# Values as the stationary operand, and inverse sums through diagonal matrices, in one attention of a two-block kernel

## The reference, cut to what matters

```python
def dense_attn(q, k, v):
    Bq, Lq, Hq, dh = q.shape
    Hk = k.shape[2]
    qg = q.reshape(Bq, Lq, Hk, Hq // Hk, dh)
    s = jnp.einsum('bqkgd,bskd->bkgqs', qg, k).astype(jnp.float32) * (dh ** -0.5)
    p = jax.nn.softmax(s, axis=-1).astype(v.dtype)
    o = jnp.einsum('bkgqs,bskd->bqkgd', p, v)
    return o.reshape(Bq, Lq, Hq * dh)
...
    y_b = blocked_attn(q, jnp.concatenate([ck, k], axis=1), jnp.concatenate([cv, v], axis=1))
    y_a = conformer_conv(a_val, a_gate, conv_w, conv_b, ln_g, ln_b)
    y = jnp.concatenate([y_a, y_b], axis=-1) * jax.nn.silu(z)
    x = x + gate * (y @ w_out)
```

## Time and profile before

| what | value |
|---|---|
| median of 3 runs | 1135.54 us (1134.69 to 1135.82) |
| profiled execution, its time | 1135.69 us |
| its span | 1133.9 us |
| TensorE busy | 1097.7 us, 97% |
| VectorE busy | 750.8 us, 66% |
| ScalarE busy | 550.6 us, 49% |
| GpSimd busy | 44.5 us, 4% |
| granted TensorE clock, mean | 0.995 |

### The profile page before, as it was taken

One profiled execution on the slowest core, in us unless ns is written; L12 is line 12 of the kernel. 1 busy time (PEld: TensorE's weight loads), 2 busy tenths in 40 slices (PEclk: granted clock), 3 DMA queues, 4 the chain that ended last, 5 costly groups with the idle time before them and its releaser, 6 DMA issues. The chain is left out here.

```text
span 1133.9 us, 17977 instructions
## 1 busy us (share of the span) xinstructions
PE 1097.7 (97%) x7052; PEld 948.2 (84%) x7052; DVE 750.8 (66%) x1456; ACT 550.6 (49%) x986; POOL 44.5 (4%) x55
## 2 busy tenths in 40 slices
PE   8999999999999999999999999999999999999996
PEld 6877879899887877889999988898876887989865
DVE  4765756655555566776888888789777653834475
ACT  5543845444444543855444444435457623623273
POOL 1000001000000000000000000100300000000000
PEclk9999999999999999999999999999999999999999
DMA  9668055555554568045556546343335037864000
GB/s 340 236 207 307 2 154 181 177 194 187 186 180 160 186 193 321 2 149 188 167 192 206 188 161 200 102 149 112 110 140 187 2 112 261 196 171 138 30 18 39
DMA packets 52536, 182.30 MB, mean 161 GB/s; under 512 B 18661, under 2 KB 31333, under 8 KB 32869
## 3 DMA queue, kind: packets, MB, share of 16 engines
q1 hardware_dynamic: 52452, 181.16, 48.5%
HBM read 178.26 MB, written 2.89 MB: 160 GB/s over the span
## 5 line engine op out<-in xcount | busy, mean ns | idle before, releaser
L224 DVE TENSOR_TENSOR w_lo<-ring,w_hi 128x1024 fp32r<-128x1024 f32 x260 | 317.1, 1224 | 214.1 <-ACT w_hi L218 211.5
L218 ACT CAST w_hi<-ring 128x1024 fp32r<-128x1024 f32 x260 | 271.5, 1052 | 323.1 <-PE banks L280 319.1
L280 PE MATMUL banks<-shared_hi,w_hi 128*128 128x256 f32 (+1 forms) x448 | 134.0, 299 | 0.0
L280 PE MATMUL banks<-shared_lo,w_hi 128*128 128x256 f32 (+1 forms) x448 | 133.7, 298 | 0.0
L280 PE MATMUL banks<-shared_hi,w_lo 128*128 128x256 f32 (+1 forms) x448 | 133.6, 298 | 0.0
L280 PE MATMUL banks<-w_hi,u_hi 128*128 128x512 f32 x256 | 100.6, 393 | 0.0
L280 PE MATMUL banks<-w_lo,u_hi 128*128 128x512 f32 x256 | 100.4, 392 | 0.0
L280 PE MATMUL banks<-w_hi,u_lo 128*128 128x512 f32 x256 | 100.3, 392 | 0.0
L280 PEld LDWEIGHTS banks<-shared_hi,w_lo 128*128 128x128 f32 x448 | 85.7, 191 | 2.6
L280 PEld LDWEIGHTS banks<-shared_hi,w_hi 128*128 128x128 f32 x448 | 85.7, 191 | 2.5
L280 PEld LDWEIGHTS banks<-shared_lo,w_hi 128*128 128x128 f32 x448 | 85.7, 191 | 2.4
(11 more groups left out here) (401 smaller groups left out, 2257.0 us busy)
## 6 DMA issues: line engine op xcount, KB each, us to landing
ring<-in_w_up SPq DMA_DIRECT2D x32, 1024.0 KB, 5.1
ring<-in_w_down SPq DMA_DIRECT2D x32, 1024.0 KB, 5.1
ring<-in_w_in SPq DMA_DIRECT2D x24, 1024.0 KB, 6.4
ring<-in_ab_ada SPq DMA_DIRECT2D x12, 1024.0 KB, 5.2
ring<-in_cd_ada SPq DMA_DIRECT2D x12, 1024.0 KB, 5.1
ring<-in_cd_in SPq DMA_DIRECT2D x12, 1024.0 KB, 8.9
ring<-in_w_out SPq DMA_DIRECT2D x8, 1024.0 KB, 6.9
ring<-in_ab_in SPq DMA_DIRECT2D x16, 512.0 KB, 4.8
```

What stands on the lines that cost most here:

```text
L218: nc.scalar.copy(w_hi[:, n % PARTS, :], part_source(key, q)).then_inc(hi_ready, 1)
L224: nc.vector.tensor_tensor(w_lo[:, n % PARTS, :], part_source(key, q), w_hi[:, n % PARTS, :].bitcast(F32), ALU.subtract).then_inc(part_read ...
L280: mm = nc.tensor.matmul(dst, a, b, start=first_one and i == 0, stop=last_one and i == 2, skip_group_check=shares_bank)
```

## The change

A new function, `attend_by_feature`, takes the place of `attend` in this one stage. What it does otherwise:

- The units are put in another order: two halves of 12, and in each the four heads of one group of tokens follow each other.
- Turning a piece is now a product: the probabilities' piece is stationary, and a 128x128 diagonal matrix with the inverse row sums moves. So the turned probabilities come out scaled. GpSimd makes the diagonal: the identity times the inverse sums, broadcast along the row; three such matrices are held, each with room for two row groups.
- The values are stationary (64 columns), and the turned, scaled probabilities move. Units i and i + 2, two heads with the same values, write to the lower and the upper 64 partitions of one bank. The result stands with features on the partitions, so nothing is left to transpose.
- TURN is 3 and VALUES 8; 4 probabilities and 6 turned ones are held; ten products of `keep_busy` stand behind the first four scores.
- VectorE no longer scales products. After the first half it gates banks 6 and 7 (features 0 and 2); the second half's are gated in `out_project`.
- "ab_out" now stands in `next_key`: its first two parts of weights are split at the end of the attention. `out_project` has no transposes, its two gates read banks 6 and 7, and casts and subtractions follow.

```diff
-        next_key = {"ab_out": "cd_in", "cd_in": "cd_out", ("ffn", DEPTH - 1): "ab_in"}
+        next_key = {"attended": "ab_out", "ab_out": "cd_in", "cd_in": "cd_out", ("ffn", DEPTH - 1): "ab_in"}
...
-                    if attended is not None:
-                        for g in range(4):
-                            for t in range(4):
-                                mm = nc.tensor.transpose(banks[:, 4 + g, t * P:(t + 1) * P],
-                                                         mixed[:, t, BANK + g * P:BANK + (g + 1) * P], ident[:])
-                            mm.then_inc(turned_here, 1)
-                    else:
+                    if attended is None:
...
-                        act.wait_ge(gate_done, g + 1)
+                        if g % 2 == 1:
+                            act.wait_ge(gate_done, g // 2 + 1)
...
-                        dve.wait_ge(turned_here, g + 1)
-                        nc.vector.scalar_tensor_tensor(out=gated_y[g], in0=banks[:, 4 + g, :], scalar=0.5, in1=silu_z[g],
+                        nc.vector.scalar_tensor_tensor(out=gated_y[g], in0=banks[:, 6 + g // 2, :], scalar=0.5, in1=silu_z[g],
...
+        def attend_by_feature(units, probs, probsT, diagonals, finals, gate_chunk, aside, aside_scalar, next_key):
...
+            SCALE, TURN, VALUES = 2, 3, 8
...
+                    def turn(i):
+                        pe.wait_ge(probs_ready, i + 1)
+                        pe.wait_ge(diagonal_ready, i + 1)
+                        if i >= 2:
+                            pe.wait_ge(turned_copied, i - 1)
+                        for r, (_, _, c0, n, _, _) in enumerate(units[i]["rows"]):
+                            for c in range(c0, c0 + n, P):
+                                mm = nc.tensor.matmul(banks[:, T + i % 2, c:c + P], probs[i % HELD][:, c:c + P],
+                                                      diagonals[i % DIAGONALS][:, r, :], start=True, stop=True)
+                        mm.then_inc(probs_turned, 1)
+
+                    def values(i):
+
+                        pe.wait_ge(turned_copied, i + 3)
+                        if i >= HALF_UNITS:
+                            pe.wait_ge(gate_done, i % 2 + 1)
+                        pair = (i, i + 2)
+                        for r in range(len(units[i]["rows"])):
+                            n_chunks = len(units[i]["rows"][r][4])
+                            for c in range(n_chunks):
+                                for u in pair:
+                                    _, _, c0, _, vs, out = units[u]["rows"][r]
+                                    mm = nc.tensor.matmul(out, vs[c], probsT[u % TURNED][:, c0 + c * P:c0 + (c + 1) * P],
+                                                          start=c == 0, stop=c == n_chunks - 1)
+                        mm.then_inc(values_ready, 1)
+
+                    scores(0)
+                    for i in range(n_units + VALUES + 2):
+                        if i % 2 == 1 and i + 1 < n_units:
+                            scores(i + 1)
+                            if i == 1:
+                                keep_busy(T + 1, 10)
+                        if i >= VALUES and i % 4 == 0 and i - VALUES < n_units:
+                            values(i - VALUES)
+                        if i >= VALUES and i % 4 == 2 and i - VALUES < n_units:
+                            values(i - VALUES - 1)
+                        if TURN <= i < n_units + TURN:
+                            turn(i - TURN)
+                    keep_busy(0, 4)
...
+                    for i in range(n_units + SCALE):
+                        w = i - SCALE
+                        if w >= 0:
+                            invert(w)
+                        if i < n_units:
+                            find_max(i)
+                        advance(more, 1)
+                        if i == HALF_UNITS + 7:
+                            for j in range(2):
+                                dve.wait_ge(values_ready, HALF_UNITS // 2 - 1 + j)
+                                gate_chunk(j).then_inc(gate_done, 1)
+                    advance(more)
+                    for q in range(AHEAD):
+                        split_lo(dve, next_key, q)
+
+                @block.gpsimd
+                def _(pool):
+                    for w in range(n_units):
+                        pool.wait_ge(inverted, w + 1)
+                        if w >= DIAGONALS:
+                            pool.wait_ge(probs_turned, w - DIAGONALS + 1)
+                        for r in range(len(units[w]["rows"])):
+                            last = nc.gpsimd.tensor_tensor(diagonals[w % DIAGONALS][:, r, :], ident[:],
+                                                           inverse[:, w % SUMS, r:r + 1].broadcast_to([P, P]), ALU.mult)
+                        last.then_inc(diagonal_ready, 1)
...
+                    for i in range(n_units + TURN):
+                        if i < n_units:
+                            exponential(i)
+                        if i >= TURN:
+                            copy_turned(i - TURN)
+                        advance(more, 1)
+                    advance(more)
+                    for q in range(AHEAD):
+                        split_hi(act, next_key, q)
```

More of the change, by code:

```diff
@@ L975, in _ @@
                         split_own(split_hi, act, key, q)
-                        if attended is not None and q == 0:
-                            high(0)
                         if attended is not None and q == 1:
-                            for g in range(1, 4):
+                            for g in range(4):
                                 high(g)
@@ L1047, in _ @@
                         if attended is not None and q == 0:
[L1048 removed]
+                            gate(1)
+                            gate(3)
                         split_own(split_lo, dve, key, q)
[L1050 to L1052 removed]
                         if attended is not None and q == 1:
[L1054 to L1058 removed]
+                            for g in range(4):
+                                low(g)
                         if beside and q == 1:
@@ L2542, in second_block @@
                     units = []
[L2543 to L2545 removed]
+                    for g in range(B_KV):
+                        pairs = [(i, kv) for i in (2 * g, 2 * g + 1) for kv in range(B_KV)]
                         vs = [[proj[:, t, AB_V0 + kv * HD:AB_V0 + (kv + 1) * HD] for t in range(4)]
                               for kv in range(B_KV)]
[L2548 to L2555 removed]
@@ new lines, in second_block @@
+                        for t in range(TT + 1):
+                            for i, kv in pairs:
+                                l, to = slice(kv * HD, (kv + 1) * HD), banks[i % 2 * HD:(i % 2 + 1) * HD, 6 + kv, :]
+                                if t < TT:
+                                    rows = [(hT[l, i, t * P:(t + 1) * P], hT[l, 4, :], 0, BANK, vs[kv],
+                                             to[:, t * P:(t + 1) * P])]
+                                else:
+                                    rows = [(hT[l, i, t2 * P:(t2 + 1) * P], hT[l, 4, SEQ:2 * SEQ], (t2 - 2) * SEQ, SEQ,
+                                             vs[kv][2:4], to[:, t2 * P:(t2 + 1) * P]) for t2 in (2, 3)]
+                                units.append({"rows": rows})
@@ L2556, in second_block, with gate_chunk @@
+                    gated_y = [proj[:, g, AB_Q0:AB_Q0 + BANK] for g in range(4)]
+                    def gate_chunk(j):
+                        return nc.vector.scalar_tensor_tensor(out=gated_y[2 * j], in0=banks[:, 6 + j, :], scalar=0.5,
+                                                              in1=silu_z[4 + 2 * j], op0=ALU.mult, op1=ALU.mult)
                     y_hi, y_lo = turned_y
```

91 lines of the change are left out of this document (68 added, 23 removed).

## The result

| what | before | after |
|---|---|---|
| time, median | 1135.54 us (1134.69 to 1136.04) | 1139.28 us of 5 runs (1138.22 to 1140.02) |
| span of the profiled execution | 1133.9 us | 1138.2 us |
| first scores of the stage to the first product of the projection | 51.69 us | 55.29 us |
| from there to the end | 227.77 us | 227.81 us |

The changed kernel takes 1.0035 times as long, with a 95% interval of 1.0023 to 1.0047: slower, by 3.7 us where 2.0 were predicted. The span grew by 4.3 us; the profiled execution of the changed kernel took 1140.02 us and was the slowest of its five. Of this 3.60 stand where the prediction looked, 0.04 behind it, and 0.66 ahead of the changed stage, in code that is the same in both kernels.

The account below looks back on a forecast made before the run. TensorE was taken as the bound: start 858.76, scores 10.6, turning 24.2 and values 12.4 end at 905.9 us. The hand-over puts the first projection product at 908.1, +2.0 us, so 1137.5 us; range 1134.5 to 1141.2.

Parts of the forecast that it names:

- The bound: The changed attention stage is bound by TensorE, without idle time in its steady part; VectorE and ScalarE have some 20% left.
- The start: At the stage's start, third scores move from 858.33 to 858.76 us; the 2.40 us of clock-keeping products mostly fill waiting.
- Values: Value products in the stage: 1.03 us a pair of units, 12.4 us in all where they took 21.1.
- Turning: Products by diagonals in place of transposes: 0.92 us a unit plus tile changes, 24.2 us where it took 11.4.
- the upper bound of 25.6: Most that the stage's turning was to cost in us, with 0.119 us an instruction and 0.14 a tile change.
- the changes of tile: About 20 of 24 turns stand before a half-array tile, taken at 0.10 us each.
- The hand-over: From attention to output projection, VectorE's weight split ends the stage; first product at 908.1 us, 2.0 later than before.
- the bound of 0.2%: For the whole kernel, 2.3 us can't be told from no change; forecast +0.18%, same 0.49, slower 0.44.
- GpSimd: Its 32 diagonal multiplications in the stage, taken at 0.5 us each, stay hidden even with a lock of 0.6 us.
- Rival 1: In the attention stage GpSimd's multiplications become the bound: 3.3 us more, 1140.8 us, from about 0.75 us each; chance 0.13.
- Rival 2: GpSimd's first multiplication in the stage meets a run of two-tensor work: 2.4 us more, 1139.9 us; chance 0.08.
- Rivals 3 and 4: Turning at its lower bound, 1133.5 us, chance 0.09; products by a diagonal costing what transposes cost, 1127.2 us, chance 0.02.

Follow-up runs that it names:

- the third experiment: The changed kernel without the ten clock-keeping products behind the first four scores; 1140.18 us.
- the fifth experiment: The changed kernel with each diagonal made by GpSimd in four pieces of 32 columns instead of one instruction; 1139.83 us.
- the first experiment: The changed kernel with turning by transposes again, diagonals still made and waited for, inverse sums left out of the result; 1129.80 us.
- the last experiment: The changed kernel, diagonals kept, with two units turned one behind the other and the first w_hi cast one step earlier; 1137.54 us, 1.0014 of the kernel before.
- sixth experiment: The changed kernel, but VectorE scales the probabilities in place, TensorE turns them by transposes and there are no diagonals; 1136.40 us.
- the second and the ninth experiment: Second: changed kernel, two units turned one behind the other, 1137.59 us. Ninth: changed kernel, GpSimd scaling, transposes turning, first w_hi cast one step earlier, 1131.21 us.
- the last three experiments: Changed kernel with an earlier cast and: GpSimd scaling with transposes, 1131.21 us; scaling shared by GpSimd and VectorE, 1129.39 us; two turns together, diagonals kept, 1137.54 us.

## Why the prediction was right or wrong

**The bound** was right. TensorE has no idle time in the steady part before or after (the earlier trace rows and the rows above), and what its stream gained or lost stood in the distance up to the first product.

**The start** was right: the third scores are 859.44 - 855.10 = 4.34 us behind the first, predicted 4.32. The idea behind it was right too, and the third experiment showed a second use that the prediction hadn't named.

**Values** were right: 1.02 to 1.03 us for a pair, predicted 1.03 from the later attention.

**Turning** is the term that was mis-sized. From the third scores to the clock-keeping products are 52.72 - 4.34 = 48.38 us. Ten pairs of scores at 1.06 and twelve of values at 1.025 take 22.9, so 24 turns take 25.5 us, predicted 24.2: 1.3 us more, just inside the upper bound of 25.6. Two errors of opposite sign stand in it.

The instruction is 0.112 us ((1.06 - 0.275) / 7 in the x8 row that follows a turn), not 0.1155. The x10 row gives 0.112 as well. The x16 row beside it stands behind scores, which use half the array:

```profile
1071.06 1.99 PE L1271 MATMUL banks<-kT_cd,qT_cd 64*128 64x512 f32 x8 [0.30 <-PEq L732]
```

So it holds 0.10 us for a change of tile, and without that it is 0.112 too. The x8 row is 0.05 us longer than this price gives; no run shows why.

And the changes of tile cost about 0.20 us a block, not 0.10. The prediction counted what leaving for a half-array tile costs (0.58 against 0.50 in the earlier trace rows), but nothing for entering. The earlier trace rows had a sign of it: four transposes take 0.50 us and are 0.66 long behind scores, 0.45 and 0.61 behind the full-array values. The prediction took these two as one price. With both mended, 24 x 8 x 0.112 + 20 x 0.20 = 25.5. The first error made turning 0.7 us too dear and the second 2.0 us too cheap. That they cancel in part is luck.

**The hand-over** was right in its mechanism, that VectorE's split ends the stage, and 0.4 us short. From the start of the last turn the copy came at +1.19 (predicted 1.2) and the casts 0.49 behind it (0.5). The second subtraction ended at +5.12, predicted 5.0: the two stand back to back for 2.36 us, so the second began when the first had ended, and not 1.09 behind its cast as reckoned. From there to the first product it was 0.44 us, not the 0.30 that stands in the earlier trace rows for a stage that TensorE ends. The last turn and the values behind it took 2.99 us, a tenth less than taken, so the chain had less of TensorE's time to hide behind. The whole, from the clock-keeping products on, is 2.57 us, predicted 2.2.

1.3 + 0.4 are 1.7 us: with 2.0 that is 3.7; values a tenth cheaper than taken make it the 3.60 that the stage with its hand-over grew by. The result lies inside the stated range. Both terms came out longer, and with them the result crossed the bound of 0.2% that the prediction stood just inside of; it had called "within 0.2%" a little likelier than "slower".

**GpSimd** was right in what mattered and 0.1 us too dear (0.40, taken 0.5). Rival 1 decides from about 0.75 us, and the fifth experiment, at 0.83 us and more, found its first wait. The prediction gave GpSimd the 0.60 us of the reduction as room; the two diagonals of a unit with two row groups need 0.76, and at 877.13 they held up an aside step. Rival 2 didn't come about: GpSimd's first multiplication stands at 858.87, and TensorE waits for none. Rivals 3 and 4 fall with the turn's 1.06 us; rival 4's own number, 0.58 for a turn, is what a transpose takes, and the first experiment is what its world would look like.

**The 0.66 us ahead of the stage** are no effect that I can name in the change. 0.33 of them stand at the very start of the kernel, where TensorE waits 0.83 us for its first input by DMA instead of 0.53, 0.08 more by 71.9 us, 0.20 between 170 and 355 us, and 0.10 between 512 and 726 us. The short stretches of lower clock don't explain it: both traces have them at 90 to 110 us (0.94 and 0.89, 0.96 and 0.87 in windows of 10 us) and at 720 to 730 us (0.84 and 0.86), and the distance doesn't grow there.

## What to carry to other kernels

Multiplying by a diagonal folds a scaling into a transpose, but in fp32 it isn't a transpose any more: it stands as two instructions a piece instead of one, 0.47 us more for a unit on the one engine that had no room, to save 32 small instructions on one that had 20% of its time left. Scale ahead of the turn instead, in place, on the engines that have room, and cut GpSimd's piece so that it fits beside a VectorE instruction that reads PSUM. When you price blocks of matmuls from rows, price the borders too, in both directions, and where ScalarE has a gap ahead of its last copy, put a cast of weights there rather than behind the copy; where the gap is missing, as in the last experiment, the cast delays the copy.

## What the runs showed of the hardware that was not expected

**Entering and leaving half-array tiles** costs a block of full-array products about 0.10 and 0.08 us by the rows; 0.21 for both, from eight blocks fewer at equal work.

**GpSimd's multiplication** with a broadcast operand takes 0.40 us at 128 columns, 0.61 at 256 and 1.04 at 512: about 0.19 us and 1.67 ns a column.

**Idle time and the clock.** A wait of 1.90 us at the start of the stage stood beside a granted clock of 0.81, one of 2.77 us ahead of the projection beside 0.92; one of 1.41 us at the same place beside none, and one of 1.59 us within the stage (sixth experiment, for the gate) beside none either. Between 720 and 730 us TensorE idles 2.05 us or more in one place in all thirteen traces: in eleven the clock of 720 to 730 us is 0.83 to 0.88, in two (the second and the ninth experiment) it is 1.00. So such an idle time mostly goes with a fall of the clock from its upper level of 2.4 GHz, but not always.

**The same code at different times.** The stage began between 852.88 and 858.11 us in the profiled executions, with the same instructions ahead of it. The windows show further stretches of lower granted clock, where TensorE is busy for 9.4 of 10 us or more, at a few places that are not the same in each: at 90 to 110 us in five of the thirteen traces, at 840 to 860 us in seven, at 440 to 450 us in one. In the last experiment:

```profile
850.00:860.00 10.00, 9.70 (x59) 6.49 (x57) 2.84 (x5) 2.38 (x5) 0.54 (x1) 0.80 0.84 318
```

TensorE is busy 9.70 of 10 us there, as in the changed kernel (9.70), where the clock is 1.00. What brings these stretches was not found. They are why edits were read by distances inside the stage, and why one run of this kernel can't settle 2 us: 23 runs of the kernel before, beside the last three experiments, lie between 1132.85 and 1139.82 us.
